# Queue orders at five waits of a two-block kernel: which engine instruction stands ahead of which

## What is computed

```python
h = rmsnorm(x, norm_mix_g[l]); proj = h @ w_in[l]
q  = rmsnorm(c_q, ...) @ mla_w_uq[l];  kv = rmsnorm(c_kv, ...) @ mla_w_ukv[l]
k_rot, q rotated (rope); r_q, r_k rotated (rope)
up = einsum('bsnw,nwd->bsnd', stack([y_a, y_b, y_c]), w_branch[l])
x = x + (sigmoid(gate_logits) * up).sum(n) @ w_out[l]
x = x + square(relu(rmsnorm(x) @ w_up[l])) @ w_down[l]
```

```python
h = h + 0.5 * g1 * (silu(hn @ w_gate) * (hn @ w_up)) @ ffn1_w_out[l]
z = modulate(rms_norm(h)) @ w_in[l] ...
```

## Time and profile before

| | |
|---|---|
| median of three executions | 2282.25 us (2279.36 to 2284.7) |
| the profiled execution, own time | 2287.89 us |
| its span, first to last instruction | 2286.0 us |
| TensorE matmuls busy | 2169.3 us (95%) |
| VectorE busy | 1417.6 us (62%) |
| ScalarE busy | 1109.6 us (49%) |
| GpSimd busy | 55.4 us (2%) |
| mean granted TensorE clock | 0.953 of full speed |
| chain that ended last | TensorE 87%, VectorE 7%, ScalarE 4% |

### The profile page before, as it was taken

One profiled execution on the slowest core, in us unless ns is written; L12 is line 12 of the kernel. 1 busy time (PEld: TensorE's weight loads), 2 busy tenths in 40 slices (PEclk: granted clock), 3 DMA queues, 4 the chain that ended last, 5 costly groups with the idle time before them and its releaser, 6 DMA issues.

```text
span 2286.0 us, 33380 instructions
## 1 busy us (share of the span) xinstructions
PE 2169.3 (95%) x13908; PEld 1939.6 (85%) x13908; DVE 1417.6 (62%) x1866; ACT 1109.6 (49%) x1757; POOL 55.4 (2%) x40
## 2 busy tenths in 40 slices
PE   8899989999989998999999989899999998989999
PEld 7788878998979887899899978689989997868998
DVE  5455647777435655877765665665566566576555
ACT  5236615444424761544455553545555554355554
POOL 0110000000001000000001000000000100000000
PEclk9999999999989999999899999889999999988999
DMA  6343256886425226789554542235545454223553
GB/s 259 108 166 107 79 208 254 355 345 274 166 74 185 93 75 233 287 344 362 211 198 166 189 143 92 74 114 182 187 164 191 175 185 141 99 74 111 184 185 129
DMA packets 56165, 409.54 MB, mean 179 GB/s; under 512 B 6608, under 2 KB 6992, under 8 KB 7888
## 3 DMA queue, kind: packets, MB, share of 16 engines
q1 hardware_dynamic: 46512, 330.20, 40.7%
q10 hardware_dynamic: 9504, 77.21, 8.5%
HBM read 406.34 MB, written 1.05 MB: 178 GB/s over the span
## 4 chain that ended last, share of the span: by engine, by line
PE 87%; DVE 7%; ACT 4%; issue 1%; DMA 1%; POOL 0%; DVEq 0%; ACTq 0%; SPq 0%; POOLq 0%
PE bank L547 25%; PE bank L548 24%; PE bank L549 24%; PE bank L950 4%; PE bank L1025 1%; PE bank L1670 1%; PE bank L836 1%; DVE weights_low L388 1%; PE bank L795 1%; DMA raw_weights<-in_stream 1%; DVE weights_low L390 1%; ACT weights_high L378 1%; PE bank L816 1%; PE bank L902 1%; ACT scratch L449 0%
## 5 line engine op out<-in xcount | busy, mean ns | idle before, releaser
L547 PE MATMUL bank<-h_high,weights_high 128*128 128x256 f32 x2944 | 858.9, 292 | 17.8 <-DVE h_low L520 13.0
L548 PE MATMUL bank<-h_low,weights_high 128*128 128x256 f32 x2944 | 846.0, 287 | 0.0
L549 PE MATMUL bank<-h_high,weights_low 128*128 128x256 f32 x2944 | 845.3, 287 | 0.0
L378 ACT ACTIVATE weights_high<-raw_weights 128x1024 fp32r<-128x1024 f32 x292 | 309.1, 1059 | 807.4 <-PE bank L549 729.7
L388 DVE TENSOR_TENSOR weights_low<-raw_weights,weights_high 128x1024 fp32r<-128x1024 f32 x292 | 365.9, 1253 | 533.4 <-ACT weights_high L378 531.8
L547 PEld LDWEIGHTS bank<-h_high,weights_high 128*128 128x128 f32 x2944 | 578.4, 196 | 37.1 <-DVE work L509 14.9
L548 PEld LDWEIGHTS bank<-h_low,weights_high 128*128 128x128 f32 x2944 | 578.6, 197 | 3.8 <-issue 1.9
L549 PEld LDWEIGHTS bank<-h_high,weights_low 128*128 128x128 f32 x2944 | 578.0, 196 | 0.0
L390 DVE TENSOR_TENSOR weights_low<-raw_weights,weights_high 128x1024 fp32r<-128x1024 f32 x292 | 358.2, 1227 | 0.0
L379 ACT ACTIVATE weights_high<-raw_weights 128x1024 fp32r<-128x1024 f32 x292 | 305.2, 1045 | 0.0
L547 PE MATMUL bank<-weights_high,hidden_high 128*128 128x512 f32 x608 | 239.1, 393 | 10.9 <-DVE hidden_low L649 8.4
(11 more groups left out here) (276 smaller groups left out, 2159.9 us busy)
## 6 DMA issues: line engine op xcount, KB each, us to landing
raw_weights<-in_stream SPq DMA_DIRECT2D x310, 1024.0 KB, 4.9
work<-in_ada ACTq DMA_DIRECT2D x64, 1152.0 KB, 9.4
consts<-in_consts SPq DMA_DIRECT2D x1, 2048.0 KB, 12.7
work<-in_row ACTq DMA_DIRECT2D x2, 836.0 KB, 4.5
x<-in_x SPq DMA_DIRECT2D x1, 1024.0 KB, 5.0
out_x<-x SPq DMA_DIRECT2D x4, 256.0 KB, 2.0
gain_row<-in_final SPq DMA_DIRECT2D x1, 512.0 KB, 13.4
vec<-in_vec SPq DMA_DIRECT2D x1, 169.0 KB, 12.7
```

The lines of the kernel that those rows point to most:

```text
L378: act.activation(high[:, 0:SPLIT], raw[:, 0:SPLIT], ACT.Copy).then_inc(m["high_a"], 1)
L547: pe.matmul(out, aH, bH, start=start, stop=False, skip_group_check=True)
L548: pe.matmul(out, aH, bL, start=False, stop=False, skip_group_check=True)
L549: return pe.matmul(out, aL, bH, start=False, stop=stop, skip_group_check=True)
```

## The change

Five places get another order; no arithmetic is changed. (1) In the first block the chunks `bq0`, `bq1`, `bk0` go ahead of `rsw0` to `psw`, on TensorE, in the banks' order and on VectorE. (2) ScalarE copies all four `uq` banks before the splits of `bv0` and `bv1`, and VectorE has their low halves behind the copies of `kv0` (`bv0`) and ahead of `qsw2` (`bv1`). (3) In the mix, VectorE takes the low part of `wc0` after the second `b2` group and each pair's low part one group later, `wc1`'s low part last; ScalarE takes the pairs' high parts ahead of `wc1`'s split. (4) At the last tile of the second block's feed-forwards the hidden tile's parts go ahead of the split of `dq`; the low halves of `dq` go ahead of, and into, the next norm. (5) `norm_low` takes a chunk's second low half after its second pair, at the first norm of every layer and at the norm ahead of `dq`.

```diff
@@ -72,8 +72,7 @@
 
 GROUPS1 = (
     [(f"n1_{b}", "V") for b in range(4)] + [("cq01", "A"), ("cq2kv0", "A"), ("kv1pe", "A"), ("rq0", "A"), ("rq1", "A"), ("rk0", "A"), ("rk1", "A"),
-     ("nc", "A")] + [(f"rsw{g}", "V") for g in range(4)] + [("psw", "V")]
-    + [(n, "A") for n in ("bq0", "bq1", "bk0", "bk1")]
+     ("nc", "A"), ("bq0", "A"), ("bq1", "A"), ("bk0", "A")] + [(f"rsw{g}", "V") for g in range(4)] + [("psw", "V"), ("bk1", "A")]
     + [(f"uq{g}", "A") for g in range(4)] + [(f"kn{g}", "V") for g in range(4)] + [("kv0", "V"), ("kv1", "V")]
     + [(f"qsw{g}", "V") for g in range(4)]
     + [(n, "A") for n in ("bv0", "bv1", "rv0", "rv1")] + [("rg0", "V"), ("rg1", "V")]
@@ -379,15 +378,19 @@
     act.activation(high[:, SPLIT:CH], raw[:, SPLIT:CH], ACT.Copy).then_inc(m["high_b"], 1)
 
 
-def split_low(dve, m, plan, i):
+def split_low_half(dve, m, plan, i, half):
 
     name = plan.split[i]
     raw, (high, low) = m.raw_slot(plan, name), m.halves(plan, name)
-    done = m.raw_done[plan.index[name] % RAW]
-    dve.wait_ge(m["high_a"], plan.at("high_a", i + 1))
-    dve.tensor_tensor(low[:, 0:SPLIT], raw[:, 0:SPLIT], high[:, 0:SPLIT].bitcast(F32), ALU.subtract).then_inc(done, 1)
-    dve.wait_ge(m["high_b"], plan.at("high_b", i + 1))
-    dve.tensor_tensor(low[:, SPLIT:CH], raw[:, SPLIT:CH], high[:, SPLIT:CH].bitcast(F32), ALU.subtract).then_inc(done, 1)
+    signal = ("high_a", "high_b")[half]
+    c = slice(half * SPLIT, half * SPLIT + SPLIT)
+    dve.wait_ge(m[signal], plan.at(signal, i + 1))
+    dve.tensor_tensor(low[:, c], raw[:, c], high[:, c].bitcast(F32), ALU.subtract).then_inc(m.raw_done[plan.index[name] % RAW], 1)
+
+
+def split_low(dve, m, plan, i):
+    split_low_half(dve, m, plan, i, 0)
+    split_low_half(dve, m, plan, i, 1)
 
 
 def at_event(split, eng, m, plan, name):
@@ -500,7 +503,8 @@
-def norm_low(dve, m, plan, k, name, gain, shift):
+def norm_low(dve, m, plan, k, name, gain, shift, weights=None):
@@ -524,6 +528,8 @@
         for b in range(4):
             m.wait_full(dve, plan, f"{name}_{b}")
             low(b)
+            if b == 1 and weights is not None:
+                split_low_half(dve, m, plan, weights, 1)
     else:
         temp(0)
         for b in range(4):
@@ -859,6 +867,8 @@
     for t in range(2):
         mm = pe.matmul(b[:, T:2 * T], m.const("ones"), latent_sq(m, 3 + t), start=(t == 0), stop=(t == 1))
     mm.then_inc(full("nc"), 1)
+    for name in ("bq0", "bq1", "bk0"):
+        pe_pair(pe, m, plan, name)
 
     for g in range(4):
         pe_begin(pe, m, plan, f"rsw{g}")
@@ -867,8 +877,7 @@
                   stop=True).then_inc(full(f"rsw{g}"), 1)
     pe_begin(pe, m, plan, "psw")
     pe.matmul(m.bank(plan, "psw")[:, 0:T], m.const("rot_mla"), latent(m, 5), start=True, stop=True).then_inc(full("psw"), 1)
-    for name in ("bq0", "bq1", "bk0", "bk1"):
-        pe_pair(pe, m, plan, name)
+    pe_pair(pe, m, plan, "bk1")
 
     pe.wait_ge(m["cqn_ready"], m.at("cqn_ready", 5))
     for g in range(4):
@@ -1092,8 +1101,7 @@
                 ins.then_inc(A, 1)
             elif g % 2 == 1:
                 ins.then_inc(m.raw_done[chunk % RAW], 2)
-        at_event(split_high, act, m, plan, name)
-    for name in ("kn3", "kv0", "kv1"):
+    for name in ("uq1", "uq3", "kv1"):
         at_event(split_high, act, m, plan, name)
     for name, v, g in (("bv0", sb_v, 0), ("bv1", sb_v, 1), ("rv0", ret_v, 0), ("rv1", ret_v, 1)):
         full(name)
@@ -1161,9 +1169,9 @@
         if name == "b0_3":
             act.wait_ge(m["y_ready"], m.at("y_ready", 2))
             ada_load(0)
-    for j in range(4):
-        act.wait_ge(m["comb_ready"], m.at("comb_ready", j + 1))
-        mix_high(act, m, comb, j)
+            for j in range(4):
+                act.wait_ge(m["comb_ready"], m.at("comb_ready", j + 1))
+                mix_high(act, m, comb, j)
     act.wait_ge(m["mix_low"], m.at("mix_low", 4))
     ada_load(1)
     at_event(split_high, act, m, plan, "wc0")
@@ -1205,10 +1213,10 @@
         at = l * NV1 + VEC1[name][0] + t
         return m.vec1[:, at:at + 1]
 
-    split_low(dve, m, plan, 0)
+    split_low_half(dve, m, plan, 0, 0)
     if l == 0:
         dve.wait_ge(m.loaded[2], 16)
-    norm_low(dve, m, plan, 0, "n1", lambda t: g1("mix", t), None)
+    norm_low(dve, m, plan, 0, "n1", lambda t: g1("mix", t), None, 0)
     split_low(dve, m, plan, 1)
     if l > 0:
         vec_mods_last(dve, m, plan.prev, step)
@@ -1230,6 +1238,8 @@
 
     cos_m, sin_m = m.trig[:, 0:T], m.trig[:, T:2 * T]
     sin_r = m.trig[:, 3 * T:4 * T]
+    for name in ("bq0", "bq1", "bk0"):
+        full(name)
     dve.wait_ge(m["trig_ready"], 1)
     for g in range(4):
         full(f"rsw{g}")
@@ -1245,10 +1255,7 @@
     dve.wait_ge(m["cos_done"], m.at("cos_done", 5))
     dve.tensor_tensor(tiles(mla_k(m, 0, HEADS)[64:96], HEADS), wide(latent(m, 5)[64:96], HEADS), wide(t1[64:96, 0:T], HEADS),
                       ALU.add).then_inc(m["key_rope_ready"], 1)
-    for name in ("bq0", "bq1", "bk0", "bk1"):
-        full(name)
-    for name in ("uq1", "uq3"):
-        at_event(split_low, dve, m, plan, name)
+    full("bk1")
     for g in range(4):
         full(f"kn{g}")
         dve.tensor_copy(mla_k(m, 2 * g, 2)[0:64], m.bank(plan, f"kn{g}")[0:64, :]).then_inc(V, 1)
@@ -1261,8 +1268,13 @@
                 ins.then_inc(V, 1)
             elif tt == 1:
                 ins.then_inc(m.raw_done[plan.index["ukv"] % RAW], 2)
-        at_event(split_low, dve, m, plan, f"kv{tt}")
+        if tt == 0:
+            at_event(split_low, dve, m, plan, "uq1")
+        else:
+            at_event(split_low, dve, m, plan, "kv1")
     for g in range(4):
+        if g == 2:
+            at_event(split_low, dve, m, plan, "uq3")
         full(f"qsw{g}")
         t1 = rope_temp(m, g + 1)
         dve.tensor_tensor(tiles(t1, 2)[0:96], tiles(m.bank(plan, f"qsw{g}")[:, :], 2)[0:96], wide(sin_m[0:96], 2),
@@ -1391,10 +1403,12 @@
         branch(0, j)
     for j in range(4):
         branch(2, j)
-    for n, name in enumerate(("b0_3", "b2_1")):
-        at_event(split_low, dve, m, plan, name)
-    for j in range(4):
-        mix_low(dve, m, comb, j, j)
+        if j == 1:
+            at_event(split_low, dve, m, plan, "b0_3")
+        if j > 0:
+            mix_low(dve, m, comb, j - 1, j - 1)
+    mix_low(dve, m, comb, 3, 3)
+    at_event(split_low, dve, m, plan, "b2_1")
     mac(0)
     at_event(split_low, dve, m, plan, "wc0")
     mac(1)
@@ -1824,9 +1838,11 @@
             act.activation(e, e, ACT.Exp).then_inc(m["fgate_exp"], 1)
             full(f"fu{n}_{j}")
             m.wait_freed(act, plan, f"fu{n}_{j}")
-            if j > 0:
+            if 0 < j < FF2_TILES - 1:
                 at_event(split_high, act, m, plan, f"fd{n}_{j - 1}")
             hidden_high(act, m, plan, f"fd{n}_", j)
+            if j == FF2_TILES - 1:
+                at_event(split_high, act, m, plan, f"fd{n}_{j - 1}")
             if j in ROWS_AT[n]:
                 r = ROWS_AT[n][j][0]
                 for half in range(2):
@@ -1989,14 +2005,14 @@
         at = l * NV2 + VEC2[name][0] + t
         return m.vec2[:, at:at + n]
 
-    split_low(dve, m, plan, 0)
+    split_low_half(dve, m, plan, 0, 0)
 
     def full(name):
         m.wait_full(dve, plan, name)
         at_event(split_low, dve, m, plan, name)
 
-    def norm(k):
-        norm_low(dve, m, plan, k, f"n{k + 1}", lambda t: modx(m, l)[:, 8 * k + t:8 * k + t + 1], lambda t: mod_col(m, 3 * k, t))
+    def norm(k, weights=None):
+        norm_low(dve, m, plan, k, f"n{k + 1}", lambda t: modx(m, l)[:, 8 * k + t:8 * k + t + 1], lambda t: mod_col(m, 3 * k, t), weights)
 
     def add(r, s, i, tt, half, bank):
         c = piece(m, tt, half)
@@ -2163,12 +2179,13 @@
         for n in {11: (0,), 13: (1, 2)}.get(s, ()):
             mix_low(dve, m, mixed, MIX_ORDER[n], n)
 
-    norm(0)
+    norm(0, 0)
     if l == 0:
         vec_mods_last(dve, m, plan.prev, step)
     split_low(dve, m, plan, 1)
     ffn(1, 0)
-    norm(1)
+    split_low_half(dve, m, plan, plan.split_index["dq"], 0)
+    norm(1, plan.split_index["dq"])
     at_event(split_low, dve, m, plan, f"fd1_{FF2_TILES - 1}")
 
     dve.wait_ge(m.rows_full, l * 16 + 16)
```

## The result

The changed kernel took 2233.11 us (median of 4 executions, 2231.57 to 2235.41) where the kernel before took 2283.47 in the same rounds: ratio 0.9775, 95% interval 0.9761 to 0.9789. That is 50.4 us faster; the forecast was 2223 in a range of 2212 to 2246.

What follows compares the result with a forecast made beforehand. Of the 2286.0 us span at most about 117 us were TensorE waits, the rest could only come from slow matmuls; 2 x (7.1 + 6.7 + 9.0 + 5.3) + 2.8 = 59.0 us less gave 2223, range 2212 to 2246.

Steps and rivals of the forecast that it cites:

- the gaps: Whole kernel: the share of the forecast gain from less TensorE idle time, 41.2 us.
- the clock terms: Behind four closed gaps per layer pair: half of each low-clock stretch saved, 2.5, 2.6, 2.1 and 1.7 us, doubled 17.8.
- B: First block, rotations behind three chunks: `psw`'s wait goes, 0.6 us new at `bk1`; gain 7.1 us a layer.
- C: First block, bank copies ahead of the `bv0` and `bv1` splits: `kv0`'s wait goes; gain 6.7 us a layer.
- D: First block's mix split branch by branch: gap of 6.9 us ahead of `wc0` and 2.1 of clock; 9.0 a layer.
- E: Second block, last hidden part ahead of `dq`'s split: 4.2 gap plus 1.7 clock less 0.6; 5.3 us a layer.
- A: Half a split moved behind the norm's first part at layer starts: shorter TensorE wait, 2.8 us in all.
- Rival 2: A tight cover fails, `wc1`'s load or `rv0` late: 1.5 to 4 us plus low clock, both layers; 2233; chance 0.17.
- Rival 1: Whole kernel: the gaps close but the low clock falls elsewhere, so 17.8 us are lost: 2241; chance 0.12.

Runs made afterwards that it cites:

- run 4: On the kernel before, only the last hidden part ahead of `dq`'s split, with `dq`'s low halves behind and inside the norm: 2281.07 us, ratio 0.9981.
- run 10: On the changed kernel, the first split of the second block's layers whole again ahead of its first norm: 2231.33 us, ratio 0.9767.
- run 9: The changed kernel once more with the same text, profiled and timed again: 2231.5 us, ratio 0.977 to the kernel before.
- run 6: On the changed kernel, both low halves of `dq` ahead of the norm's modulation instead of one there and one inside: 2222.48 us, ratio 0.9729.
- run 7: On the changed kernel, both low halves of `dq` moved from VectorE to GpSimd: 2234.26 us, ratio 0.9783.

## Why the prediction was right, and where it missed

The direction, the range and the closing of the gaps held; the clock terms held in their sum and not part by part. The miss of the median is 10 us: 8.6 of gain that did not come (59.0 against 50.4), 1.2 since the kernel before ran at 2283.5 in these rounds.

**The gaps.** Right: 41.2 forecast, 40.7 found in the first profile and 37.7 in the second, so the half microsecond is luck. By parts alone the idle time fell by 4.8 (B), 9.3 (C), 10.7 (D), 5.8 (E) and 0.5 (A), 31 in all. Most of what is missing is not theirs: the line of the scores, which no part touches, stood at 12.8, 11.3, 12.8, 13.9 and 12.7 us in these five traces against 11.4 before, 6.5 more in all. Another 1.0 is the wait that B alone moves to `kv0`, which C closes.

**B: "Gain 34.7 - 26.9 - 0.6 = 7.1".** The chunk, the rotations and the wait of 0.6 at `bk1` came as written (0.84; VectorE's addition took 1.67 beside GpSimd). Alone it gave 10.3 of 14.2; what was missing is 1.0 us at `kv0`, 1.4 at the scores, and clock (low time 5 us less, not 11). The Trainium skill ("SBUF — State Buffer", "The single rule") has VectorE with two inputs in SBUF and GpSimd exclude each other for a whole instruction, and by that each addition could have been 1.5 us late. VectorE's timeline of the changed kernel beside the GpSimd row:

```profile
617.55 1.67 DVE L1250 TENSOR_TENSOR work<-work,scratch 128x512 f32<-128x512 f32 x1 [0.69 <-POOL work L1506]
...
619.85 1.04 DVE L1250 TENSOR_TENSOR work<-work,scratch 128x512 f32<-128x512 f32 x1
...
623.24 0.69 DVE L1250 TENSOR_TENSOR work<-work,scratch 128x512 f32<-128x512 f32 x1
```

```profile
616.17 5.88 POOL L1506 TENSOR_TENSOR work<-work,trig 128x512 f32<-128x512 f32 x4 [499.18 <-PE bank L876]
```

The addition took 1.67 and 1.04 us while GpSimd ran and 0.69 once it had ended, so the trace agrees with a blocked wait, and its price was 0.35 to 1.0 us an addition, not 1.5. The GpSimd products kept their pace (5.88 against 5.81 in the earlier trace rows).

**C: 6.7.** Right: 13.0 of 13.4 for two layers, with low time 10 us less as the term had it. ScalarE's timeline shows what is left of the wait for the load, with no copy behind it any more:

```profile
641.62 1.06 ACT L377 ACTIVATE weights_high<-raw_weights 128x1024 fp32r<-128x1024 f32 x1 [2.74 <-DMA raw_weights<-in_stream]
```

It was 4.47 in the earlier trace rows.

**D: 9.0, margin 0.8 at `wc1`.** Right in its time, 19.5 for 18.0, in part by luck: idle time fell by 10.7 and not 13.8 (the scores took 1.4, the waits for L462 at the norms 1.4, those for low weight halves 0.9), and low time by 18 us where the term had 8. The margin was real. VectorE's and ScalarE's timelines at the mix:

```profile
856.42 1.47 DVE L1025 TENSOR_TENSOR h_low<-work,h_high 128x512 fp32r<-128x512 f32 x2
858.15 2.36 DVE L388 TENSOR_TENSOR weights_low<-raw_weights,weights_high 128x1024 fp32r<-128x1024 f32 x2 [0.26 <-ACT weights_high L377]
```

```profile
856.54 0.63 ACT L1019 ACTIVATE h_high<-work 128x512 fp32r<-128x512 f32 x1 [2.01 <-DVE work L1385]
857.08 1.04 ACT L377 ACTIVATE weights_high<-raw_weights 128x1024 fp32r<-128x1024 f32 x1
```

The first low half of `wc1` is done at about 858.15 + 1.2 = 859.4; TensorE starts `wc0` at 854.57 and takes 5.44 us, so it comes at 860.0. Rival 2 stood 0.6 us away from deciding. It was the engines' order and not the load that set this: ScalarE starts on `wc1` straight after the fourth high part, with no wait.

**E: "Gain 4.2, and half of the 3.5 us at low clock", less 0.6.** This is the term that failed: 3.3 us instead of 10.6 for both layers. The gap and the 0.7 at the norm were right, the sign of the clock term was wrong: 18 us more low time instead of 7 less. The step that failed is taking the stretch behind the gap as saved: it went, and those behind the norm and in the mixer grew by as much each (run 4). Rival 1 ("the low clock falls elsewhere") was the right reading for this part and for A, half right for B, and wrong for C and D (low time 191 and 183 us against 201).

**A: 2.8.** The wait shrank by 1.1 as written and the time did not: 1.2 alone, 0 in company. The step that failed is counting a microsecond less of waiting as a microsecond less of time: low time rose by 9 us alone, and in company idle time did not even change (79.1 and 79.0 in runs 10 and 9).

**The clock terms as a whole.** 17.8 forecast, 14.4 in the profiled pair (20.6 with the second profile of the changed kernel). But the profile of before was an execution with the lowest clock of all (0.953, against a median of 0.956), 14 us of low time above the middle; a gain read from it was partly the luck of that execution. With it goes that the spans differ by 55.1 and the medians by 50.4. Two profiles of the one kernel (run 9) differ by 6.2 us in TensorE's busy time and, the other way, by 3.0 in idle time. The Trainium skill ("TensorE: Matmul & The Clock Gate", "What's actually happening") says that the number of slow matmuls varies from run to run with the phase of a free-running count, and the traces agree that it varies: 0.51 and 0.68 for the same stretch of the same kernel. The phase itself no row here shows.

**A sign that was there before.** Against rival 1 the prediction held that all four low stretches have a gap ahead, and it named a low stretch without one as a sign of being wrong. That sign is in the trace of before and in that of the changed kernel. The windows just ahead of the mixer's low stretches (those of 13.7 and 17.1 us in runs 4 and 9), before and after, and the last matmul ahead of the second:

```profile
1411.20:1417.60 6.40, 6.40 (x53) 6.18 (x51) 1.98 (x2) 0.00 (x0) 0.00 (x0) 1.00 0.45 165
```

```profile
1356.00:1362.40 6.40, 6.40 (x45) 5.96 (x43) 3.70 (x7) 1.33 (x3) 0.00 (x0) 1.00 0.26 58
```

```profile
1362.29 0.25 PE L557 MATMUL bank<-weights_high,h_low 128*128 128x4 f32 x1
```

TensorE counts as busy for all of the 6.4 us, at last with matmuls of only four columns, and the clock falls all the same. In the trace of before 9 of 31 low stretches (68 of 215 us) begin so, with TensorE counted busy throughout the 6 us ahead; in the first trace of the changed kernel 9 of 22 (79 of 178 us). The four low stretches of the earlier trace rows were picked behind gaps and did not show this. So a good part of the low time never hung on a gap right ahead of it.

**What stays open.** That the low clock at the norms comes from idle TensorE there is shown: filling the gaps, with no other change, takes some 45 us of it away at these six places. What brings it in the mixer and behind the other stretches without a gap is not; no run changed the narrow matmuls. Nor is it shown why an idle time of 3.3 us ahead of `dq` is followed by less low clock than one of 2.2 (run 6), and why E and A alone raise it. All are small shifts of when the work arrives.

## What to carry to other kernels

Read a gap that is a queue's order as its full length: the four named ones went whole, 41.2 us, for 1.7 us of new waits. Before crediting a low stretch to the gap ahead of it, look whether other low stretches have no gap ahead. Read the clock behind it from several executions, and give a shift of a microsecond near a norm an unknown sign of several. A wait that can't be removed can be filled: fillers sized to the wait were worth 7 to 11 us here, the same as keeping `dq`'s split whole; neither was tried with the other.

## What the runs showed of the hardware

- GpSimd's weight halves (a `tensor_tensor` of two SBUF tiles) beside VectorE's `tensor_scalar` with one SBUF tile as input (L465, 128x512 float32) held it up: up to 2.57 us for one instead of 0.48. The halves took 2.52 us each on GpSimd, all four alike; whether that is a hold-up too, no run shows. The row of the norm lines of run 7, and of the changed kernel (duration ns min/median/max):

```profile
L465 DVE TENSOR_SCALAR work<-x,small x40: 473/481/2572, 8.3 to 2033.3; 128x512 f32<-128x512 f32 x40
```

```profile
L465 DVE TENSOR_SCALAR work<-x,small x40: 477/481/489, 8.2 to 2031.8; 128x512 f32<-128x512 f32 x40
```

- The Trainium skill ("SBUF — State Buffer", "The single rule") names `tensor_scalar` among the operations that can take the ports that VectorE shares with GpSimd. These rows agree; the expectation of run 7 had put L465 beside GpSimd as harmless but for its last rival.
- The granted clock fell to half while TensorE counted as busy without a gap, behind matmuls of four columns: 1.00 over the 6.4 us ahead, then 0.51 for 17.1 us (rows above).
- Executions of one kernel differ by 4 to 15 us, and their clock goes with it: 0.965 at 2228.5 us and 0.972 at 2215.27 us in run 6.
